# Left operand tiles of a matrix kernel fetched in pairs: one 512 KB transfer and one semaphore for two of four places

## What is computed

```python
h = rms_norm(x, norm_pre)
u_s, z_s, q, k, v, z_r, gl_s, gl_r = jnp.split(h @ w_in, SPLIT_IDX, axis=-1)
y_s = s5_mixer(u_s, ...) * jax.nn.silu(z_s)        # has g @ w_glu inside
y_r = retention(q, k, v) * jax.nn.silu(z_r)
m = (jax.nn.sigmoid(gl_s) * (y_s @ w_proj_s5)
     + jax.nn.sigmoid(gl_r) * (y_r @ w_proj_ret))
x = x + rms_norm(m @ w_out, norm_post)
```

## Time and profile before

| what | value |
|---|---|
| median of 3 runs | 2218.93 us (2218.14 to 2222.05) |
| the profiled execution | 2220.81 us, span 2219.0 us |
| PE | 98% busy, 10288 matmuls |
| DVE | 81% |
| ACT | 52% |
| mean granted TensorE clock | 0.996 |

### The profile page before, as it was taken

One profiled execution on the slowest core, in us unless ns is written; L12 is line 12 of the kernel. 1 busy time (PEld: TensorE's weight loads), 2 busy tenths in 40 slices (PEclk: granted clock), 3 DMA queues, 4 the chain that ended last, 5 costly groups with the idle time before them and its releaser, 6 DMA issues.

```text
span 2219.0 us, 28662 instructions
## 1 busy us (share of the span) xinstructions
PE 2178.1 (98%) x10288; PEld 1806.1 (81%) x10288; DVE 1793.0 (81%) x2921; ACT 1163.5 (52%) x1961; POOL 127.6 (6%) x201
## 2 busy tenths in 40 slices
PE   8999999999999999999999999999999999999996
PEld 6687888888888888888888888988888888788885
DVE  5998997977898887886877866767788889986768
ACT  6644445455665554464555554845545545455554
POOL 6044001000000000000000000200000000000000
PEclk9999999999999999999999999999999999999998
DMA  9577568685585465689774989576846755744557
GB/s 374 224 234 250 156 225 278 232 297 197 176 283 191 156 215 168 194 305 298 256 220 139 316 254 304 153 240 211 286 147 195 247 176 190 256 151 135 185 165 275
DMA packets 268815, 496.61 MB, mean 224 GB/s; under 512 B 51920, under 2 KB 60112, under 8 KB 265984
## 3 DMA queue, kind: packets, MB, share of 16 engines
q1 hardware_dynamic: 221408, 409.55, 56.1%
q10 hardware_dynamic: 37568, 50.44, 6.5%
q0 software_dynamic: 9696, 34.78, 5.0%
HBM read 378.29 MB, written 116.39 MB: 223 GB/s over the span
## 4 chain that ended last, share of the span: by engine, by line
PE 81%; DVE 10%; DMA 3%; POOL 2%; issue 2%; SPq 2%; ACT 1%; DVEq 0%; ACTq 0%; POOLq 0%
PE psum L2025 59%; PE psum L2022 18%; DMA araw<-aops 2%; DVE a_lo L1464 2%; DVE b_lo L1466 2%; POOL work L788 1%; DVE work L1727 1%; DVE work L1420 1%; PE psum L2045 1%; DVE work L1780 1%; DMA work<-in_xT 1%; DMA keep<-m3d 0%; PE psum L2128 0%; PE psum L2063 0%; PE psum L2081 0%
## 5 line engine op out<-in xcount | busy, mean ns | idle before, releaser
L1018 ACT ACTIVATE a_hi<-araw 128x512 fp32r<-128x512 f32 x644 | 405.9, 630 | 854.1 <-PE psum L2025 610.6
L1464 DVE TENSOR_TENSOR a_lo<-araw,a_hi 128x512 fp32r<-128x512 f32 x644 | 444.1, 690 | 320.1 <-ACT a_hi L1018 317.0
L2025 PE MATMUL psum<-a_hi,b_hi 128*128 128x512 f32 x2352 | 632.8, 391 | 9.1 <-ACT b_hi L1027 7.6
L2025 PE MATMUL psum<-a_lo,b_hi 128*128 128x512 f32 x2352 | 632.6, 391 | 4.2 <-DVE a_lo L1464 3.7
L2025 PE MATMUL psum<-a_hi,b_lo 128*128 128x512 f32 x2352 | 629.3, 389 | 0.0
L2025 PEld LDWEIGHTS psum<-a_hi,b_hi 128*128 128x128 f32 x2352 | 441.3, 188 | 104.0 <-ACT b_hi L1027 7.3
L2025 PEld LDWEIGHTS psum<-a_lo,b_hi 128*128 128x128 f32 x2352 | 441.2, 188 | 101.9 <-DVE a_lo L1464 10.0
L2025 PEld LDWEIGHTS psum<-a_hi,b_lo 128*128 128x128 f32 x2352 | 442.1, 188 | 92.4
L1466 DVE TENSOR_TENSOR b_lo<-bx,b_hi 128x512 fp32r<-128x512 f32 x432 | 297.7, 689 | 0.0
L1027 ACT ACTIVATE b_hi<-bx 128x512 fp32r<-128x512 f32 x432 | 266.4, 617 | 0.9 <-DMA bx<-in_wstream 0.7
L2022 PE MATMUL psum<-b_hi,a_lo 128*128 128x512 f32 x672 | 180.4, 390 | 4.4 <-DVE a_lo L1464 4.4
(11 more groups left out here) (190 smaller groups left out, 1576.4 us busy)
## 6 DMA issues: line engine op xcount, KB each, us to landing
araw<-aops SPq DMA_DIRECT2D x632, 256.0 KB, 3.2
bz<-in_wstream SPq DMA_DIRECT2D x224, 256.0 KB, 4.6
aops<-work SPq DMA_DIRECT2D x28, 1024.0 KB, 6.7
spill<-keep ACTq DMA_DIRECT2D x28, 1024.0 KB, 5.8
bx<-in_wstream SPq DMA_DIRECT2D x108, 256.0 KB, 4.9
by<-in_wstream SPq DMA_DIRECT2D x108, 256.0 KB, 5.3
work<-spill SPq DMA_DIRECT2D x20, 1024.0 KB, 7.5
aops<-work POOLq DMA_DIRECT2D x15, 1024.0 KB, 5.8
```

What stands on the lines that cost most here:

```text
L1018: A.activation(a_hi[:, r, :], left(s), ACT.Copy, scale=gain).then_inc(head, 1)
L1464: V.tensor_tensor(a_lo[:, r, :], left(s), a_hi[:, r, :].bitcast(F32), ALU.subtract).then_inc(split, 1)
L2025: done = T.matmul(bank, b[:, r, cols], a[:, r, :], start=first and part == 0, stop=last and part == 2, skip_group_check=on)
```

## The change

Left tiles are loaded two at a time. `load_a(s)` does nothing at an odd s. At an even s it waits until the tile of step s-3 (before: s-4) has been split and issues one DMA for the tiles of s and s+1, 128x2x512 elements, 512 KB, into two neighbouring places. The four semaphores of the places become two, one for each pair of places, and ACT waits for the pair's semaphore. The 12 tiles of glu that come from `turned` keep one DMA each; the two of a pair are issued one behind the other. `a_transfers` counts what has been issued on a semaphore. All that stood behind `load_a` in an odd step now stands there without a left tile in front.

```diff
+def a_transfers(s):
+    pair = s // 2
+    return sum(2 if by_step_loads(*place(2 * q)[:2]) else 1 for q in range(pair % 2, pair + 1, 2)
+               if place(2 * q)[0] not in (GU, GO0))
...
             def load_a(s):
                 g, p, k = place(s)
+                if s % 2:
+                    return
                 if s >= A_RING:
-                    sp.wait_ge(split, 2 * (s - A_RING + 1))
-                dst = araw[:, s % A_RING, :]
+                    sp.wait_ge(split, 2 * (s + 1 - A_RING + 1))
+                done = a_loaded[s // 2 % 2]
...
-                    src = aops[ops_of(g) + TILES[g] * p + k]
-                sp.dma_start(dst, src).then_inc(a_loaded[s % A_RING], 16)
+                    first = ops_of(g) + TILES[g] * p + k
+                    sp.dma_start(araw[:, s % A_RING:s % A_RING + 2, :], op_block(first, 2)).then_inc(done, 16)
...
-                    act.wait_ge(a_loaded[s % A_RING], 16 * a_loads(s))
+                    act.wait_ge(a_loaded[s // 2 % 2], 16 * a_transfers(s))
```

More of the change, by code:

```diff
@@ L108, in s_order, with by_step_loads @@
     return 32 + 2 * order + ((1 - k // 4) if p == S1 else k // 4) + 1
-def a_loads(s):
-    return (s - 7 * 8 * (1 if s < BASE[GO0] else 2)) // A_RING + 1
+def by_step_loads(g, p):
+    return g == GGLU and p in (A11, A12, A22)
+def a_transfers(s):
+    pair = s // 2
+    return sum(2 if by_step_loads(*place(2 * q)[:2]) else 1 for q in range(pair % 2, pair + 1, 2)
+               if place(2 * q)[0] not in (GU, GO0))
 def sums_before(g, p, k):
@@ L303, in build_program @@
         op_stored = {p: sem(f"op_stored{p}") for p in (A11, S4, S3, A12, A22)}
-        a_loaded = [sem(f"a_loaded{r}") for r in range(A_RING)]
+        a_loaded = [sem(f"a_loaded{r}") for r in range(A_RING // 2)]
         bx_loaded = [sem(f"bx_loaded{k}") for k in range(8)]
@@ L524, in load_a @@
                 if g == GGLU and p in (A11, A12, A22):
-                    i, j = (1, 4 + k) if p == A22 else (0, 4 + k if p == A12 else k)
-                    src = turned[8 + j].rearrange("(t q c) -> q t c", t=STEP, q=P)[:, :, HC * i:HC * i + HC]
-                    dst = dst.rearrange("p (t c) -> p t c", t=STEP)
+                    for n in range(2):
+                        i, j = (1, 4 + k + n) if p == A22 else (0, 4 + k + n if p == A12 else k + n)
+                        src = turned[8 + j].rearrange("(t q c) -> q t c", t=STEP, q=P)[:, :, HC * i:HC * i + HC]
+                        sp.dma_start(araw[:, (s + n) % A_RING, :].rearrange("p (t c) -> p t c", t=STEP), src).then_inc(done, 16)
                 else:
```

## The result

| what | before | after |
|---|---|---|
| median | 2220.11 us (4 runs) | 2256.54 us (4 runs, 2254.01 to 2259.11) |
| span of the profiled execution | 2219.0 us | 2252.8 us |
| after / before | | 1.0165, 95% interval 1.0153 to 1.0178 |

The change costs 36.4 us by the medians, 33.8 us between the two traces. The forecast was +8.9 us and at most 18.4: slower was right, the size was not. Where a later run is compared with the changed kernel, the traces can differ from the medians by some 4 us, since each trace is of one execution.

What follows compares the result with a forecast made beforehand. The prediction took PE, busy 98% of the span, as the bound. Its eight terms summed to +8.9 us, which on the median of 2218.93 us gave 2227.8 us, with a range of 2217 to 2237 us.

Steps and rivals of the forecast that it cites:

- Term 8: out1, steps 709 and 710: 2 MB of x now stand in front of the pair of 710; +0.6 us.
- Term 7: wr0, step 596: same pattern as Term 6, the even tile's lateness reaches PE; +2.1 us.
- Term 6: ws1, step 568: behind DVE's gate product no lead is left, so the even tile's lateness reaches PE; +2.0 us.
- term 5: Steps 442 to 445: the pair puts the tile of 443 ahead of the retention's tables, a gain; -0.9 us.
- Term 3: zr, steps 118 to 123: SP's issues queue up, and odd left tiles now precede right tiles; +1.2 us.
- terms 2 and 3: The first is steps 78 to 81, a late pair with no right tile sharing SP's queue, +1.0 us; the second is Term 3.
- Term 4: Start of gr0: the new order puts two more right tiles in front of the pair of 424; +2.5 us.
- the list of late places: Places where PE was expected to lose or gain: 64, 78 to 81, 118 to 123, gr0's start, 442 to 445, 568, 596, out1.
- the spare lead of 4.0 us: Quiet stretches: ACT starts a tile 5.2 us before PE where 1.2 are needed, so 4.0 us of lateness is absorbed.
- the ring closes: Rival: pairs release their places late, so loads fall behind by more each turn; 34 us slower, 2253 us, chance 0.08.

Runs made afterwards that it cites:

- hybrid: The changed kernel with pairs in only 368 of the 644 steps, the quiet stretches, and single loads released as before elsewhere; 2220.73 us.
- two_both: two_own, with ACT also waiting at the even step for both tiles of the pair; 2258.61 us.
- two_own: The kernel before, with both tiles issued at the even step after one wait, as two 256 KB DMAs on the four old semaphores; 2237.57 us.
- after_spread: The changed kernel with POOL's 15 stores to `m1d` spread out instead of issued in two bursts; 2242.58 us.
- after_early: The changed kernel with each pair released one split count earlier, at the `a_lo` of step s-3 instead of `b_lo`; 2237.18 us.
- late_even: The kernel before, single loads kept, with the even step's left load waiting for the split of step s-3 instead of s-4; 2243.22 us.

## Why the forecast was right in sign and wrong in size

**What held.** PE was the bound and the only way was up. Quiet stretches cost nothing that hybrid shows. ACT's waits were 101, about 100 forecast. The median landing was 4.0 us (3.8 to 4.5 forecast). Term 8 measured 1.2 against 0.6. Term 7 measured 2.2 against 2.1, but 1.8 of it at 592, four steps before the 596 that it named, so the figure is partly luck. Term 6 had the right mechanism, a late tile with DVE's gate product behind it, and nearly the right size (2.5 against 2.0), but it struck one block earlier, at 564: DVE had the product behind the split of 562.

```profile
1695.31 0.69 DVE L1472 TENSOR_TENSOR a_lo<-araw,a_hi 128x512 fp32r<-128x512 f32 x1 [3.80 <-ACT a_hi L1026]
1695.99 0.69 DVE L1474 TENSOR_TENSOR b_lo<-bx,b_hi 128x512 fp32r<-128x512 f32 x1
1696.60 4.21 DVE L1735 TENSOR_TENSOR work<-work,keep 128x2048 f32<-128x2048 f32 x1
```

At 443 the tables no longer stood in front and PE did not wait (-0.9, term 5), but 444 then paid 1.1, inside the ends given. The Trainium skill's rule on batching, in "DMA: Bandwidth & Descriptors", gave no gain that the intervals show: 2 us in 2256 between two_both and the change. The page gives its fit for transfers that GpSimd issues, which the prediction leaves out; these loads are SP's.

**What failed: the method for the late places.** "Both tiles of a pair land when the odd one landed before, plus 0.7." At 78 this gave 239.6; it was 244.40. The odd tile's landing of 7.4 us had been read as a fixed time; it came of the share that a load gets beside POOL's stores, and a load of twice the bytes, issued 1.5 us later, took 11.4 us. In two_own, where nothing is joined, the second tile of the pair took 10.6 us and the first 7.3. The windows of before showed the DMA engines at 0.96 there, and the stores stand in POOL's timeline at 230.08; I looked for company in SP's queue only ("no right tile shares SP's queue there"). Term 3 has the same fault: it puts the lateness down to SP's queue, and before, the tile of 119, issued at 352.51 and landed at 365.50, lay behind the eight stores that POOL issued from 348.62 on. after_spread moves the stores away and with them goes the loss of terms 2 and 3, of which 5.6 and 2.7 us are error.

**The price of landing together.** The prediction priced the wait for both tiles at the time of 256 KB, 0.7 us a pair, and the pair's single semaphore at nothing. two_both against two_own puts this wait at 21 us.

**"A loss is not added to the next one if both lie in one stretch."** That held for a shift of everything. It did not hold for SP: a pair that is late delays the split that releases the next one. gr0 lost 2.2, then 2.1, 0.6, 0.5, and 1.8 more up to 433. Term 4, with its surroundings, was 5.0 short. Its start was a pair from `turned`, of which the prediction says "this moves nothing"; in hybrid, where these tiles are single, ACT waits 1.7 us for the tile of 419, much as before (1.6). A small shift of the release counts for much: 0.6 us was worth 19 in after_early.

**Places not looked at.** 168, 336, 372 to 376 and 534 were not on the list of late places: 7.7 us. At 534 ACT had waited 2.96 us for its tile before, so that place could have been on it; at the others it had not waited. At 336 the spare lead of 4.0 us did not count, since PE waited there for work of DVE that stands in order behind the left tile's.

**The clock.** Three idle times (78, 118, 336) were followed by the lower clock, 1.7 us each, 5.1 us in all. This is part of the figures above, at 336 together with the 0.9 us that PE no longer waits. No term had this price.

**The rival "the ring closes"** named 2253 us, near the result, for a loss of 1.6 us in 21 pairs. Its core, that a turn's release hangs on the landing before it, is seen in gr0. Its picture is not: by hybrid it closes nowhere outside the crowded stretches, and a third of the loss sits at two bursts of stores. That ACT waits for both tiles was no rival of its own and should have been: two_own and two_both put 21 us on it, late_even 24 on the later issue, the order in the queue gives 5.7 back and the joined DMA 2: 37 in all, within what the runs differ by.

**What stays open.** In gr0 the trace shows the release holding the pair of 422 and SP's row that of 424, but no run parts the two in us. What made 168, 372 to 376 and 534 late was not tested. Nor was the obvious way out, a ring with more than four places.

## What to carry to other kernels

A ring of four places with one tile each has three tiles in flight while one is in use; in pairs it has one pair. Before joining transfers in such a ring, look at where the DMA engines are full by any queue, stores of other engines too, and take the landing of the joined load there as the time its bytes need beside that traffic. Then look at what else waits in order behind the consumer of the late tile: DVE's copies at 336, its work on whole blocks at 419 and 564. And release a place by the last operation that reads it: here one DVE operation, 0.6 us, was worth 2 us to single tiles and 19 to pairs.

## What the runs showed of the hardware

- After idle times of PE of 4.68, 3.82 and 2.77 us (steps 78, 118, 336 of the changed kernel) the granted clock fell to 0.50 for about 3.5 us of work and cost 1.7 us each, 36 to 61% on top of the idle time. The length of an idle time does not tell whether this follows: after 1.89 us (step 419) the clock stayed at 1.00 in the changed kernel and fell to 0.50 in two_both, and it fell after 2.15 us in two_own (422) but stayed after 2.68 in late_even (119) and 2.70 in after_spread (444).
- A load of 512 KB took 3.7 us with the stores spread and 11.4 us beside seven stores to `m1d` from POOL's queue. 256 KB took 2.5 us when issued ahead of them and 7.4 us when issued among them. In the stretch from 232 to 244, 168 to 289 GB/s moved at a DMA share of 0.77 to 0.98, less than the 353 GB/s at a share of 1.00 of the earlier trace rows: the engines were busy, but moved fewer bytes.
- Two loads of 256 KB issued one behind the other, waited for together, and one load of 512 KB differ by 2 us in 2256, over 316 pairs, no more than the intervals leave open.
